# Gate and up projections of a hybrid decoder layer: token blocks side by side in two or three banks

## The reference

```python
a = rmsnorm(x, g_mix)
u = a @ w_in                       # projection to mLSTM heads, gates and a short convolution
...                                # chunkwise mLSTM, short convolution
x = x + jnp.concatenate([h_m, y_c], axis=-1) @ w_out
f = rmsnorm(x, g_ffn)
x = x + (jax.nn.silu(f @ w_gate) * (f @ w_up)) @ w_down
e = rmsnorm(pe @ w_ple, g_ple)
x = x + jax.nn.sigmoid(x @ w_pg) * e
```

## Time and profile before

| | us |
|---|---|
| device time, median of 3 runs | 2775.99 |
| lowest and highest run | 2769.67, 2776.66 |
| profiled execution: span, first to last instruction | 2763.6 |
| TensorE matmul busy | 2677.8 |
| TensorE weight load busy | 2409.6 |
| VectorE, ScalarE, GpSimd busy | 703.5, 751.8, 795.7 |
| DMA, share of 16 engines in its largest queue | 20.4% |

### The profile page before, as it was taken

One profiled execution on the slowest core, in us unless ns is written; L12 is line 12 of the kernel. 1 busy time (PEld: TensorE's weight loads), 2 busy tenths in 40 slices (PEclk: granted clock), 3 DMA queues, 4 the chain that ended last, 5 costly groups with the idle time before them and its releaser, 6 DMA issues.

```text
span 2763.6 us, 37564 instructions
## 1 busy us (share of the span) xinstructions
PE 2677.8 (97%) x14623; PEld 2409.6 (87%) x14623; DVE 703.5 (25%) x1296; ACT 751.8 (27%) x1355; POOL 795.7 (29%) x633
## 2 busy tenths in 40 slices
PE   7999999999999999999899999969999999999998
PEld 5788878788888888878799999969999999999998
DVE  5112241311111122233620323304111111113153
ACT  5332332412121211123443233214121212111143
POOL 2223344222222222222244333422222222232222
PEclk8999999999999999999999999989999999999999
DMA  6421131111111111113121112371111111111111
GB/s 184 128 52 38 38 114 46 46 46 46 46 51 47 46 46 46 46 54 108 39 84 54 38 38 66 92 39 47 46 47 46 47 46 47 46 46 46 46 50 74
DMA packets 251139, 159.87 MB, mean 58 GB/s; under 512 B 32945, under 2 KB 242129, under 8 KB 250641
## 3 DMA queue, kind: packets, MB, share of 16 engines
q1 hardware_dynamic: 241664, 153.91, 20.4%
q10 hardware_dynamic: 9360, 4.33, 0.5%
HBM read 139.95 MB, written 18.27 MB: 57 GB/s over the span
## 4 chain that ended last, share of the span: by engine, by line
PE 90%; issue 3%; SPq 2%; DVE 2%; POOL 1%; ACT 1%; DMA 1%; POOLq 0%; DVEq 0%; ACTq 0%
PE bank L553 28%; PE bank L556 28%; PE bank L557 28%; SPq L340 2%; POOL wlo L1820 1%; PE bank L585 1%; PE bank L674 1%; DVE AL L1597 1%; PE bank L608 1%; PE bank L607 1%; PE bank L654 0%; DMA wraw<-w_ple 0%; DVE AL L1694 0%; PE bank L612 0%; PE bank L723 0%
## 5 line engine op out<-in xcount | busy, mean ns | idle before, releaser
L553 PE MATMUL bank<-AH,whi 128*128 128x352 f32 (+1 forms) x3400 | 1206.3, 355 | 19.6 <-DVE wide L1638 5.0
L556 PE MATMUL bank<-AL,whi 128*128 128x352 f32 (+1 forms) x3400 | 1196.3, 352 | 0.0
L557 PE MATMUL bank<-AH,wlo 128*128 128x352 f32 (+1 forms) x3400 | 1195.2, 352 | 0.0
L1820 POOL TENSOR_TENSOR wlo<-wraw,whi 128x1024 fp32r<-128x1024 f32 x218 | 530.2, 2432 | 1509.8 <-ACT whi L947 1509.4
L553 PEld LDWEIGHTS bank<-AH,whi 128*128 128x128 f32 x3400 | 642.8, 189 | 90.4 <-issue 12.8
L556 PEld LDWEIGHTS bank<-AL,whi 128*128 128x128 f32 x3400 | 643.2, 189 | 59.4
L557 PEld LDWEIGHTS bank<-AH,wlo 128*128 128x128 f32 x3400 | 642.0, 189 | 60.1
L947 ACT ACTIVATE whi<-wraw 128x1024 fp32r<-128x1024 f32 x218 | 230.0, 1055 | 522.2 <-PE bank L553 480.4
L553 PE MATMUL bank<-hid,whi 128*128 128x352 f32 (+1 forms) x960 | 338.8, 353 | 30.8 <-POOL wlo L1820 25.5
L556 PE MATMUL bank<-hid,whi 128*128 128x352 f32 (+1 forms) x960 | 337.1, 351 | 0.0
L557 PE MATMUL bank<-hid,wlo 128*128 128x352 f32 (+1 forms) x960 | 336.8, 351 | 0.0
(11 more groups left out here) (220 smaller groups left out, 1485.8 us busy)
## 6 DMA issues: line engine op xcount, KB each, us to landing
wraw<-w_in SPq DMA_DIRECT2D x50, 512.0 KB, 3.9
wraw<-w_gate SPq DMA_DIRECT2D x44, 512.0 KB, 3.8
wraw<-w_up SPq DMA_DIRECT2D x44, 512.0 KB, 3.8
wraw<-w_down SPq DMA_DIRECT2D x44, 512.0 KB, 3.4
wraw<-w_out SPq DMA_DIRECT2D x16, 512.0 KB, 4.1
wraw<-w_pg SPq DMA_DIRECT2D x16, 512.0 KB, 4.0
next_x<-stored_x SPq DMA_DIRECT2D x1, 4224.0 KB, 13.2
wide<-stored_x SPq DMA_DIRECT2D x2, 2112.0 KB, 9.5
```

What stands on the lines that cost most here:

```text
L553: first = nc.tensor.matmul(o, hi[:, k, cols_], mh, start=k == 0, stop=False)
L556: nc.tensor.matmul(o, hi[:, k, cols_], ml, start=False, stop=False)
L557: last = nc.tensor.matmul(o, lo[:, k, cols_], mh, start=False, stop=k == kc - 1)
L1820: nc.gpsimd.tensor_tensor(wlo[p][:, :], wraw[p][:, :], whi[p][:, :], ALU.subtract).then_inc(lo_done, 1)
```

## The change

Gate and up no longer call `product` for one block after the other, but `shared_product` once for a slab. It waits until the banks of all blocks are free. Then for each k it issues the high weights for block 0 (high, low), block 1 (high, low), and block 2 where there is one, and after them the low weights for each block. So neighbouring matmuls have the same weights, four or six in a row for `whi` and two or three for `wlo`, and the banks of a slab all get their last matmul at its end. `full` is raised per bank as before. The down projection and every other product stay with `product`. The first slab's waits for normalised data now come in the order k, block.

```diff
+            def shared_product(q, nos, bk, p, ready):
+                hi = whi[p][:, :].rearrange("p (k n) -> p k n", k=KC)
+                lo = wlo[p][:, :].rearrange("p (k n) -> p k n", k=KC)
+                outs = []
+                for b, (b0, bl) in enumerate(q.blocks):
+                    pe.wait_ge(free[bk + b], nos[b])
+                    outs.append(bank[bk + b][:, 0:bl])
+                for k in range(KC):
+                    for b, (b0, bl) in enumerate(q.blocks):
+                        if ready:
+                            ready(b, k)
+                        first = nc.tensor.matmul(outs[b], hi[:, k, :], AH[:, k, b0:b0 + bl], start=k == 0, stop=False)
+                        if b == 0 and k == 0:
+                            first.then_inc(slab_begun, 1)
+                        nc.tensor.matmul(outs[b], hi[:, k, :], AL[:, k, b0:b0 + bl], start=False, stop=False)
+                    for b, (b0, bl) in enumerate(q.blocks):
+                        last = nc.tensor.matmul(outs[b], lo[:, k, :], AH[:, k, b0:b0 + bl], start=False, stop=k == KC - 1)
+                        if k == KC - 1:
+                            last.then_inc(full[bk + b], 1)
...
                 def up_chunk(f, s, p, first):
                     for w in range(2):
                         slab_ready(s + w)
-                        for b in range(nb):
-                            product(q, f.take(3 * w + b), 3 * w + b, (p + w) % 2, KC, 0, b, begins=b == 0,
-                                    ready=normed_ready if first and w == 0 else None)
+                        shared_product(q, [f.take(3 * w + b) for b in range(nb)], 3 * w, (p + w) % 2,
+                                       normed_ready if first and w == 0 else None)
```

## The result

| | before | after |
|---|---|---|
| runs timed in turn on the same chip | 14 | 14 |
| median, us | 2774.41 | 2784.45 |
| lowest to highest, us | 2767.16 to 2779.57 | 2779.17 to 2793.32 |
| span of the profiled execution, us | 2763.6 | 2783.2 |

The ratio is 1.0042, interval 1.0031 to 1.0054: slower by 8.6 to 15 us. The two medians by themselves are 10.0 us apart. The forecast was 2780.0 (2768 to 2790). The time lies in the range; but the prediction drew the line between "same" and "slower" at 0.3%, and by that line the kernel is slower, which it had given 15 in 100 against 80 for "same". And the intervals between matmuls changed, which it had named as what would make it wrong.

The account below looks back on a forecast made before the run. The prediction took the kernel as a stream of matmuls on TensorE, its interval set by columns streamed. Its terms, 2.2 + 0.6 + 0.4 + 0.2 + 0.6 = 4.0 us, put the median of 2776.0 at 2780.0 us, range 2768 to 2790.

Parts of the forecast that it names:

- what would make it wrong: Gate and up were to keep 0.232 and 0.159 us per matmul; another interval than in the down projection would refute the prediction.
- Weight loads: 0: Gate and up: every matmul brings its load even when weights repeat, so none goes; gain taken as 0.
- The interval goes with the columns, so reordering costs nothing: Matmul stream: the interval follows columns streamed, 0.2321 us at 512 and 0.1590 at 352; the change streams the same columns.
- Banks: 0, at most 10 us: Gate and up: 3520 bank changes where there were 220; cost taken as 0, upper bound 3300 x 0.003 = 10 us.
- the rival (3 ns, 2790): Gate and up: bank changes cost time; at 3 ns each 10 + 4 us, giving 2790; 13 in 100.
- Gate slabs: 0: Gate slabs: Silu of block 0 starts up to two blocks later, but the next weights are still ready in time; cost 0.
- First slab of a group: 0.2: At k = 0 all blocks' normalised data is wanted; second group waits for block 2, 0.5 us less 0.3 back; cost 0.2.
- Down projections: Block 0's `hid` comes later: second group 2.2 us (four chunks), 0.56 (two); first group nothing (four), 0.38 (two).
- the 0.16 us to spare: First group, four-chunk down projection: PE can go on at T + 1.93, the slot is T + 2.09, so no stop.
- the rival of the small stops: Down projections: first group's spare time is missed and a low part meets GpSimd's subtraction; 8 + 4 us, 2788; 6 in 100.
- Seven were named: Sign: PE's waits at line 553 for line 1676 go from two to seven, five new of some 0.3 us, second group.
- Turns of the loop: 0.6: Second group's three loop turns: two more bank waits ahead of the slab cost 0 to 3 us; taken as 3 x 0.2.

Follow-up runs that it names:

- 2: Kernel after, but block after block into one bank, per k high, low, high weights, so no weights repeat; single time 2764.84 us.
- 3: Kernel after, but block after block into one bank, high weights three times per k, low weights left out; single time 2770.25 us.
- 9: Kernel after with its moving operands and banks, but high and low weights alternate from matmul to matmul; single time 2772.36 us.
- 10: Kernel after, but k outside, a block's three terms together, all with high weights, low part left out; single time 2762.54 us.
- 4: Kernel after, but per k each of the three terms is issued for all blocks, changing bank with every matmul; single time 2787.38 us.
- 6: Kernel after, but k outside, a block's three terms together, and 24 matmuls in a row into one bank; single time 2767.78 us.
- 5: Kernel after, but operands block after block as before the change, the bank changing every third matmul; single time 2772.35 us.
- 1: Kernel after, but per k the three terms of each block together, so the bank changes every third matmul; single time 2769.25 us.
- 7: Kernel after, but gate's first slab per loop turn and up's last before each down projection use `product` again; single time 2783.62 us.
- 8: The change in the first group (two blocks) only, second group as before; median 2774.92 us, ratio 0.9994 to the kernel before.
- 11: The change in the second group (three blocks) only, first group as before; median 2778.93 us, ratio 1.0032 to the kernel before.

## Why the prediction held, and where it didn't

*Weight loads: 0.* Right, and now tested both ways at both widths (2, 3, 9, 10). A load of 188 ns comes with each matmul, repeated or not.

The Trainium skill (Perfetto Trace Analysis, "Identifying the Most-Contended Engine") judges TensorE's headroom by MFU (the arithmetic done as a share of the peak) and the LDWEIGHTS busy share. Taken alone, that share does not mark the limit here: it is 100% at 352 columns and 81% at 512 (32.55 of 40 us in the window above), and the interval goes with the columns at both; it was 100% in the second group before and after, while the interval moved by 1.3%. What fewer loads would give no run shows.

*The interval goes with the columns, so reordering costs nothing.* This step failed. "The change streams the same columns" is true and not enough: at one width the interval also depends on the order. With two blocks it fell by 1.6 ns, 2112 x 1.6 = 3.4 us gained; with three it rose by 2.1 ns, 3168 x 2.1 = 6.7 us lost. The row was read from one order only (rows 4 and 5), and was taken for a property of the shape. That the time still lies in the range is in part luck: the two errors have opposite signs, and half of the 6.7 us is paid back by the first group.

*Banks: 0, at most 10 us.* Right for two blocks, where a change with every matmul (4) and none in 24 (6) give the same 230.6, and for a change every third matmul at both widths (5). For three blocks it is not settled. The loss is 9 x 2.1 = 19 ns a k with six changes, which would be 3.2 ns a change, just the size of the rival (3 ns, 2790). Against it: at 512 columns the same pattern costs nothing, and the same 161.1 stands in stretches that change the bank every third matmul (1, 10) and in the kernel before, in its slab after the stop at 2023.92. The order of the kernel after into one bank would have told; it was not run.

*Gate slabs: 0.* Nothing new in the waits: apart from PE's own issue and the free bank at the first slab, no wait of PE at line 573 is listed after.

*First slab of a group: 0.2.* Measured: a stop of 0.9 us in each group, less the stop of 0.36 and 0.21 ahead of the up slab that vanishes, some 1.2 us. The mechanism was another one. The wait for block 2's data did not show, because the free waits now stand together at the front, and bank 1 had just been filled by the embedding product. The prediction held that PE's sequencer is ahead and the waits therefore free, and asked only how early the sequencer is, not when the bank is: it is free at 509.28, 0.8 after the slot. 7 removes the stop by taking the banks one at a time; 5 and 6 keep it with the waits in front, whatever follows.

*Down projections.* The best part. Four chunks, second group: the matmul at 1989.71 is 0.31 late and the next 0.10 more, some 0.43 at the four in the loop and 0.49 at the fifth, against 0.44 predicted. Two chunks: a stop of 1.35 where it was 0.80, +0.55 (predicted 0.56). First group, two chunks: 1.47 where it was 0.91, +0.56 against 0.38; four chunks 0.1 each (0.18 at the fifth), against none. Here the spacing of VectorE's work was mis-sized: 0.61 us from one multiplication to the next, read where a low part followed, measured (599.34 - 597.95) / 2 = 0.70. The first low part so starts at T + 1.36 instead of T + 1.19, and the 0.16 us to spare are gone; the restart of 0.1 us follows, as the rival of the small stops had it. The timeline, VectorE and PE:

```profile
597.95 1.29 DVE L1693 TENSOR_TENSOR sl<-sl,bank 128x512 f32<-128x512 f32 x2 [19.45 <-PE bank L578]
597.98 0.39 PE L553 MATMUL bank<-hid,whi 128*128 128x512 f32 x1
...
599.34 1.29 DVE L1697 TENSOR_TENSOR hid<-sl,hid 128x512 fp32r<-128x512 f32 x2
...
600.08 0.50 PE L553 MATMUL bank<-hid,whi 128*128 128x512 f32 x1
...
600.42 0.39 PE L556 MATMUL bank<-hid,whi 128*128 128x512 f32 x1
```

The waits of PE after:

```profile
PE bank L573 <- issue: 3.9, 4, 1.1
...
PE bank L553 <- DVE hid L1697: 3.0, 5, 1.3
...
PE bank L573 <- ACT wide L1216: 0.7, 1, 0.7
```

Seven were named; five are in this row, and the timeline shows all seven.

*Turns of the loop: 0.6.* 1.20, 1.19 and 1.24 where there were 1.15, 0.91 and 1.17, so 0.4. It is not shown that the change costs this: in 8, whose second group keeps the old order, the same three are 1.32, 1.33 and 1.11, more than after.

The sum by these: first group -3.4 + 0.5 + 0.6 + 0.6 = -1.7, second 6.7 + 0.7 + 2.2 + 0.55 + 0.4 = 10.6; 8.9 us, where the lengths give 8.6. The stops come to 5.6 of it, where 4.0 were predicted. The two interval terms add 3.3 and were missing. Both the sum and the ratio's interval (8.6 to 15 us) put the change just beyond the 0.3% line. What may lie between these 8.6 us and the ratio's middle of 11.7 is not located. The dip of the clock may be a part: five profiled executions have the second group in the order of the kernel after or of 4 (after, 4, 7, 9, 11), and three of them have it; of the nine others none has. At 1.5 us each that would be about 1 us, and so few executions can also fall so by chance.

## What to carry to other kernels

An interval read from one order of matmuls is a fact of that order: before reordering a stream that is bound by TensorE, measure the new order by itself at each block width. Here 1.3% of one group's interval cost 6.7 us, more than all new stops together (5.6). Issuing the same weights again saves nothing here, so sharing weights is no reason to interleave blocks. If blocks are interleaved, keep the three terms of a block together: in experiments 1, 6 and 10 that gave the shorter interval at 512 columns and 158.9 ns in 100 of 132 slabs at 352 (161.1 in the rest), and in 1 hardly a new stop at the down projections. Keep the waits for banks where each bank is first used, and let the first block's bank fill early where a consumer stands right behind.

## What the runs showed of the hardware

- The three-block stream knows two sequences of intervals; in experiment 1 each repeats after 18 matmuls (two k). Differences of the starts in the trace, in ns, from the matmul at the given time on:

```
before, 2040.5  155 159 161 162 156 161 155 159 161 161 156 161 155 159 161 162 ...
before, 2024.2  159 159 164 162 164 159 158 159 165 161 164 160 158 159 164 162 ...
exp. 1, 1918.7  156 161 155 159 161 161 156 161 155 159 161 162 156 160 155 160 ...
exp. 1, 2328.6  165 161 164 160 158 159 164 162 164 159 159 159 164 162 164 159 ...
after,  1918.7  161 161 160 158 159 164 165 159 160 161 162 162 164 166 160 158 ...
```

  The mean of the one is 159.0, of the other 161.1. A stream enters the second after some stops at a turn of the loop. The order of the kernel before leaves it within a slab or two, that of experiment 1 keeps it until the next down projection, and the order of the kernel after is in one like it from its first slab on, with or without a stop ahead. Why there are two, and what an order does to them, is open: the runs show that weights are not it, and at 512 columns that banks are not it.
- The first matmul after a stop took 0.10 us more than a slot (1989.71 to 1989.98 instead of 0.16).
- The granted clock fell to 0.50 for some 3 us in single executions, in a stretch where the same engine was busy without a stop in others at 1.00; each time costs 1.5 us. All three dips (4, 7, 11) begin some 1 us behind the end of the same 18 one-column matmuls of the second group, which take 2 us in all; the other executions have these too, and no dip. Why it came in these three is open.
